# Last recurrent head: the low parts of six mixed tiles move from VectorE to GpSimd, and two output tiles are filled side by side

## The reference, cut to what matters

```python
def hgrn2_mixer(q_raw, f_raw, i_raw, g_raw, lb, norm_g):
    ...
    k = (1.0 - lbf) * jax.nn.sigmoid(-z)
    q = jax.nn.silu(q_raw.astype(jnp.float32))
    v = i_raw.astype(jnp.float32)
    ...
    def chunk_step(state, inp):
        qb, kb, vb, lfb = inp
        b = jnp.cumsum(lfb, axis=2)
        diff = jnp.where(causal, b[:, :, :, None, :] - b[:, :, None, :, :], -jnp.inf)
        scores = jnp.einsum('bhtk,bhsk,bhtsk->bhts', qb, kb, jnp.exp(diff))
        o = (jnp.einsum('bhts,bhsv->bhtv', scores, vb)
             + jnp.einsum('bhtk,bhkv->bhtv', qb * jnp.exp(b), state))
        ...
    o = o * lax.rsqrt(jnp.mean(o * o, axis=-1, keepdims=True) + RMS_EPS)
    o = o.reshape(B, S, HGRN_WIDTH) * norm_g.astype(jnp.float32)
    o = o * jax.nn.silu(g_raw.astype(jnp.float32))
...
    x = x + jnp.concatenate([y_pool, y_hgrn], axis=-1) @ w_out[l]
```

## Time and profile before

| | |
|---|---|
| median of 3 runs | 2525.26 us (2523.75 to 2525.31) |
| the profiled execution | 2528.88 us |
| its span in the trace | 2527.1 us |
| mean granted TensorE clock | 0.994 of full speed |
| TensorE busy | 2480.5 us, 98% of the span |
| VectorE, GpSimd, ScalarE busy | 67%, 45%, 32% |

### The profile page before, as it was taken

The page is one execution under the profiler, slowest core; times in us unless marked ns, Lnnn a source line. Parts: engine busy times, 40 slices in busy tenths (PEclk is TensorE's granted clock), DMA queues, the critical chain, the costliest instruction groups (busy, mean ns, idle before and its releaser), DMA issues.

```text
span 2527.1 us, 38526 instructions
## 1 busy us (share of the span) xinstructions
PE 2480.5 (98%) x14121; PEld 2036.5 (81%) x14121; DVE 1693.6 (67%) x1822; ACT 807.4 (32%) x1137; POOL 1133.0 (45%) x665
## 2 busy tenths in 40 slices
PE   8999998999999999999999999999999999999998
PEld 7788886878888788887877778888878888878886
DVE  6755556753334566668777879454789999986665
ACT  5333344343333000003233331311355445431003
POOL 2322222367876233323322223233379999962333
PEclk9999998999999999999999999999999999999998
DMA  6111112234424322221311101113222222243222
GB/s 211 42 42 33 33 33 93 100 113 122 134 100 148 126 99 92 100 100 42 126 40 40 39 26 50 50 44 132 84 83 83 91 75 91 84 158 108 100 94 81
DMA packets 221471, 217.48 MB, mean 86 GB/s; under 512 B 16304, under 2 KB 185947, under 8 KB 220379
## 3 DMA queue, kind: packets, MB, share of 16 engines
q1 hardware_dynamic: 189604, 122.92, 16.1%
q10 hardware_dynamic: 31798, 93.64, 10.0%
HBM read 167.24 MB, written 51.06 MB: 86 GB/s over the span
## 4 chain that ended last, share of the span: by engine, by line
PE 87%; DVE 8%; ACT 2%; issue 1%; DMA 1%; ACTq 0%; DVEq 0%; SPq 0%
PE psum L849 28%; PE psum L1134 27%; PE psum L868 21%; PE psum L1350 3%; PE psum L888 2%; PE psum L976 1%; PE psum L1279 1%; PE psum L1454 1%; DVE h_lo L2144 1%; DVE sq_sum L2412 1%; PE psum L1260 1%; DVE sq_sum L2139 1%; PE psum L1035 0%; DVE sq_sum L2546 0%; DVE x_t L2420 0%
## 5 line engine op out<-in xcount | busy, mean ns | idle before, releaser
L753 POOL CAST w_hi<-w_raw 128x1024 fp32r<-128x1024 f32 x136 | 152.7, 1123 | 1187.0 <-issue 629.7
L2448 DVE TENSOR_TENSOR x_t<-x_t,psum 128x512 f32<-128x512 f32 x416 | 284.4, 686 | 206.9 <-PE psum L868 198.4
L755 POOL TENSOR_TENSOR w_lo<-w_raw,w_hi 128x1024 fp32r<-128x1024 f32 x136 | 345.8, 2543 | 10.9
L849 PE MATMUL psum<-h_hi,w_hi 128*128 128x512 f32 x1040 | 334.3, 403 | 7.7 <-DVE h_lo L2247 6.5
L849 PE MATMUL psum<-h_lo,w_hi 128*128 128x512 f32 x1040 | 322.6, 392 | 0.0
L849 PE MATMUL psum<-h_hi,w_lo 128*128 128x512 f32 x1040 | 321.6, 390 | 0.0
L849 PEld LDWEIGHTS psum<-h_hi,w_lo 128*128 128x128 f32 x1040 | 196.1, 189 | 42.1
L849 PEld LDWEIGHTS psum<-h_lo,w_hi 128*128 128x128 f32 x1040 | 196.1, 189 | 41.9
L849 PEld LDWEIGHTS psum<-h_hi,w_hi 128*128 128x128 f32 x1040 | 190.0, 189 | 49.1 <-issue 11.8
L868 PE MATMUL psum<-down_hi,w_hi 128*128 128x512 f32 x512 | 200.3, 391 | 2.8 <-DVE x_t L2448 2.6
L868 PE MATMUL psum<-down_lo,w_hi 128*128 128x512 f32 x512 | 199.9, 390 | 0.0
(11 more groups left out here) (448 smaller groups left out, 5558.6 us busy)
## 6 DMA issues: line engine op xcount, KB each, us to landing
w_raw<-in_w_in SPq DMA_DIRECT2D x124, 256.0 KB, 3.2
w_raw<-in_w_down SPq DMA_DIRECT2D x108, 256.0 KB, 2.7
w_raw<-in_w_up SPq DMA_DIRECT2D x76, 256.0 KB, 3.9
act_rows<-mlp_a ACTq DMA_DIRECT2D x32, 512.0 KB, 3.9
down_in<-act_rows ACTq DMA_DIRECT2D x32, 512.0 KB, 3.7
ffn_raw<-in_w_up SPq DMA_DIRECT2D x44, 256.0 KB, 3.5
ffn_rows<-ffn_gate ACTq DMA_DIRECT2D x22, 512.0 KB, 2.6
ffn_in<-ffn_rows ACTq DMA_DIRECT2D x22, 512.0 KB, 3.9
```

The source lines that it names most:

```text
L753: pool.tensor_copy(hi, w_raw[:, slot, :]).then_inc(weight_hi, 1)
L755: pool.tensor_tensor(lo, w_raw[:, slot, :], hi.bitcast(F32), ALU.subtract).then_inc(weight_split, 1)
L849: last = pe.matmul(psum[:, first_bank + t, :], w, a[:, k, t * HALF:(t + 1) * HALF], start=(k == 0 and j == 0), stop=(k == KT - 1 and j == 2))
L2448: dve.tensor_tensor(x_d, x_d, psum[:, 4 + g % 4, :], ALU.add).then_inc(down_added, 1)
```

## The change

Six low parts (tiles 1 to 6) leave VectorE and go to GpSimd, in its list ahead of the split of output tile 2's weights. VectorE keeps tile 0 (right after level 1) and tile 7. ScalarE's high parts are spread over the levels, its gate (`sg_t`) moves from before level 2 to after level 4, and the copy `v_tok` goes ahead of level 4 with tile 3 before it. On VectorE `take_g` moves from behind `move(1)` to behind `merge(1, 5)`, and the product `gated` to behind `merge(3, 5)`; `move(2)` now stands ahead of the diagonal's merge. TensorE fills output tiles 0 and 1 side by side in slots 1 to 6. The number of steps in slots 1 to 3 (eight), 4, 5, 6 and 7 is the same as before. Heads 0 to 4 keep their order.

```diff
@@ GpSimd, split(n, slot, _, skipped)
                 elif isinstance(n, int) and n in (T_OUT1 + 2, T_OUT1 + 3):
+                    if n == T_OUT1 + 2:
+                        for d in range(1, KT - 1):
+                            pool.wait_ge(mix_hi_ready, d + 1)
+                            pool.wait_ge(mix_split, d)
+                            pool.tensor_tensor(h_lo[:, d, :], mix1[:, d, :], h_hi[:, d, :].bitcast(F32), ALU.subtract)\
+                                .then_inc(mix_split, 1)
@@ TensorE
             def begin_rest():
-                begin_out(1, range(5, 7))
+                for t in range(2):
+                    begin_out(t, [6])
                 begin_out(2, range(7))
-            head(HEADS - 1, [lambda: project_g(HEADS - 1), lambda: begin_out(0, range(0, 4)),
-                             lambda: begin_out(0, range(4, 7)), lambda: begin_out(1, [0]), lambda: begin_out(1, [1]),
-                             lambda: begin_out(1, [2, 3]), lambda: begin_out(1, [4]), begin_rest])
+            def begin_both(tiles):
+                for t in range(2):
+                    begin_out(t, tiles[t])
+            head(HEADS - 1, [lambda: project_g(HEADS - 1), lambda: begin_out(0, [0]),
+                             lambda: begin_both(([1, 2], [0, 1, 2])), lambda: begin_both(([3], [3])),
+                             lambda: begin_out(0, [4]), lambda: begin_both(([5], [4])),
+                             lambda: begin_out(1, [5]), begin_rest])
@@ ScalarE, head(h, last), after level(0) and level(1)
-                act.wait_ge(y_ready, h + 1)
-                act.wait_ge(zg_ready, h + 1)
-                act.activation(sg_t[:, :], zg[:, :], ACT.Sigmoid).then_inc(g_gate, 1)
                 if last:
                     act.wait_ge(tile_done, T_OUT1)
-                begin_mix(0, 1)
-                level(2)
-                begin_mix(2, 3, 4, 5, 6)
-                level(3)
...
+                    begin_mix(0, 1)
+                    level(2)
+                    begin_mix(2)
+                    level(3)
+                    begin_mix(3)
+                    values()
+                    level(4)
+                    gate()
+                    begin_mix(4)
+                    level(5)
+                    begin_mix(5, 6)
+                    level(6)
                     act.wait_ge(mix_split, KT - 1)
                     act.dma_start(x_t[:, 0:KT - 1, :].rearrange("p d t -> p (d t)"),
...
@@ VectorE, head(h, last): the branch of the last head
+                if last:
+                    mix_lo(0, 0, mix1)
+                    move(2)
+                    merge_diagonal()
+                    merge(0, 4)
+                    move(3)
+                    merge(1, 5)
+                    take_g(h)
+                    move(4)
+                    merge(2, 4)
+                    move(5)
+                    merge(3, 5)
+                    gated()
+                    move(6)
+                    merge(4, 6)
+                    merge(5, 4)
+                    merge(6, 5)
...
             head(HEADS - 1, True)
+            dve.wait_ge(mix_split, KT - 1)
             mix_lo(0, KT - 1, mix1)
```

More of the change, by code:

```diff
@@ L1583, in head, with gate, values @@
                 act.wait_ge(kd_start, h + 1)
+                def gate():
+                    act.wait_ge(y_ready, h + 1)
+                    act.wait_ge(zg_ready, h + 1)
+                    act.activation(sg_t[:, :], zg[:, :], ACT.Sigmoid).then_inc(g_gate, 1)
+                def values():
+                    act.wait_ge(v_turned, h + 1)
+                    act.activation(v_tok[:, :, :].rearrange("p c v -> p (c v)"), banks(6), ACT.Copy).then_inc(v_ready, 1)
                 level(0)
                 level(1)
-                act.wait_ge(y_ready, h + 1)
-                act.wait_ge(zg_ready, h + 1)
-                act.activation(sg_t[:, :], zg[:, :], ACT.Sigmoid).then_inc(g_gate, 1)
                 if last:
                     act.wait_ge(tile_done, T_OUT1)
-                begin_mix(0, 1)
-                level(2)
-                begin_mix(2, 3, 4, 5, 6)
-                level(3)
-                act.wait_ge(v_turned, h + 1)
-                act.activation(v_tok[:, :, :].rearrange("p c v -> p (c v)"), banks(6), ACT.Copy).then_inc(v_ready, 1)
-                if last:
+                    begin_mix(0, 1)
[10 more added lines that the diff above has]
+                    level(6)
                     act.wait_ge(mix_split, KT - 1)
@@ L1604, in head @@
                                   x_spill[:, 0:(KT - 1) * SEQ]).then_inc(x_back, 16)
-                level(4)
-                level(5)
-                level(6)
+                else:
+                    gate()
+                    level(2)
+                    level(3)
+                    values()
+                    level(4)
+                    level(5)
+                    level(6)
                 act.wait_ge(kd_turned, h + 1)
@@ L2290, in merge, with gated @@
                        .then_inc(level_merged, 1)
[L2292 to L2295, removed]
+                def gated():
+                    dve.wait_ge(g_gate, h + 1)
+                    dve.tensor_tensor(sg_t[:, :], zg[:, :], sg_t[:, :], ALU.mult).then_inc(sg_ready, 1)
                 dve.wait_ge(q_gate, h + 1)
@@ L2304, in head @@
                 move(1)
[L2305 to L2318, removed]
+                if last:
[15 more added lines that the diff above has]
+                    merge(6, 5)
+                else:
+                    take_g(h)
+                    merge_diagonal()
+                    merge(0, 4)
+                    move(2)
+                    merge(1, 5)
+                    gated()
+                    move(3)
                     dve.wait_ge(k_ready, h + 1)
                     take_f(h + 1)
[L2322 to L2329, removed]
+                    merge(2, 4)
+                    move(4)
+                    merge(3, 5)
+                    move(5)
+                    merge(4, 6)
+                    move(6)
+                    merge(5, 4)
                     take_q(h + 1)
-                merge(6, 5)
+                    merge(6, 5)
                 chunk_decay = 2 * SEQ - (2 * SEQ >> LEVELS)
```

## The result

Over 8 runs each, the median went from 2525.45 to 2532.41 us. The ratio of the changed kernel to the one before is 1.0021, 95% interval 1.0012 to 1.0029; a later series (6 runs of the changed kernel, 19 of the one before) gave 1.0030, 1.0018 to 1.0042. Taken together, the two intervals say that the change makes the kernel slower, by 3 to 11 us (0.1 to 0.4%); the forecast of 2532 us, slower, holds.

A forecast was written before the change was run, and what follows sets the result against it. It took the last head to be bound by the start of `o`, behind VectorE's ladder. `o` 6.1 us late by turns with GpSimd, plus 1 us of clock, made 7 us: 2525.26 + 7 = 2532 us, range 2528 to 2537.

The forecast's parts named there:

- What bounds the head: Last head: the start of `o`, 428.85 us before, sets the head's end, which moves by as much.
- The turns: VectorE instructions reading two SBUF tiles and GpSimd instructions alternate; a move of 1.4 us takes 6.1 at level 2.
- The layout: Hand-made schedule of the last head's ladder: last move ends at 427.5 instead of 420.7 us, `o` starts at 435.0.
- 4.9 us too long: Level 5's move between GpSimd's low parts 4 to 6, ending at 418.6 us, takes this much more.
- The clock's share: TensorE at half clock for steps behind the turning of `kd_t`: 0 to 3 us, taken as 1.
- The free edits: Spread high parts, later reload (issued at 419.9 us, landing 12.6 later) and two tiles side by side cost nothing.
- The idle time: TensorE in the last head: some 17 us idle instead of 11.4, with some 5, 5 and 3 us stretches.
- No port cost: Rival, chance 0.07: six low parts run beside the moves; `o` 6 to 9 us earlier, 2518 us.
- VectorE keeps the port through a move: Rival, chance 0.11: GpSimd waits until a move is through; `o` 4 to 6 us earlier, 2520 us.
- Cancelling: Rival, chance 0.09: earlier start and VectorE's shorter list weigh as much as the turns; within 5 us, 2525 us.
- Slower still: Rival, chance 0.11: idle time before the turning brings the clock down through `o` and the mean; 2537 to 2541 us.
- within 0.2%: Chance 0.30 that the median stays within 5 us of before, 2520.2 to 2530.3 us.

The follow-up runs named there:

- e2: The changed kernel with GpSimd's splits of `w_out` tiles 2 and 3 held until `kd_t` is turned: `o` after 41.6 us, ratio to before 1.0002.
- e3: The changed kernel's order on all engines, but low parts 1 to 6 back on VectorE: `o` after 40.9 us, ratio to before 0.9996.
- e6: The kernel before, with only GpSimd's splits of `w_out` tiles 2 and 3 held until `kd_t` is turned: `o` after 37.2 us, ratio 0.9982.
- e1: The changed kernel with GpSimd's six low parts left out, only their counts given: `o` after 35.3 us, ratio to before 0.9984.
- the repetition: The changed kernel once more, unaltered, for a second profile: median 2532.36 us, `o` after 47.6 us.
- e7: The changed kernel with each of GpSimd's six low parts replaced by a `memset` of the same tile: `o` after 36.9 us, timed once, 2525.96 us.
- e8: e5 with the low part of `w_out` tile 1's weights also held until the move of level 2 is done: `o` after 32.3 us, ratio 0.9966.
- e5: The changed kernel with all low parts on VectorE, re-placed, and `w_out` splits 2 and 3 held until `kd_t` is turned: `o` 34.4 us, ratio 0.9978.

## Why the prediction was right

- **What bounds the head.** Right: the start of `o` carried the end. It moved by 7.3 us (428.85 to 436.11), the first addition behind the head by 7.3 and 7.0. The experiments' medians rise with it (only the kernel before and e2 are out of order, by 0.5 us): 32.3, 34.4, 35.3, 37.2, 40.9, 40.9, 41.6 and 48.3 us of head go with 2515.8, 2519.3, 2521.0, 2521.4, 2524.3 (e3), 2525.3 (before), 2524.8 and 2532.4 us. One step was read wrongly: in the kernel before, the turning did not wait for the ladder's last move but for TensorE's own work at half clock, 1.3 us longer (e6). It did not matter for the sum, since in the changed kernel the turning did wait for VectorE.
- **The turns.** Right, and the core of it. The layout had the ladder's last move at 427.5 us, measured 426.6; level 2 with low parts 1 and 2 at 394.1 to 400.2, measured 394.0 to 399.8 (`qd_t` came just ahead of low part 1, so that `kd_t` and `decays` were the ones that waited, not `qd_t` and `kd_t`); `o` at 435.0 without and 436 with the clock, measured 436.1. In the changed kernel's last head too GpSimd went next wherever both waited. e1, e2 and e3 show it by removal: 13.0, 6.7 and 7.4 us of head, each with the 2.0 us of clock; they overlap and don't add up. The prediction's "4.9 us too long" for level 5 does not follow from its own times, which give 5.8 (ready at 411.5, 1.3 us of work, done at 418.6); measured are 5.7. The sum did not use it.
- **The clock's share.** Taken as 1 us inside 0 to 3, measured 2.0. The term was too small, and the ladder's was too large by 0.9; that they cancel to within 0.1 us is luck.
- **The free edits.** Right as far as the profile shows: the reload was issued at 418.15 us, landed 11.2 us later, and nothing behind the head waited for it; idle time before the first addition was 5.21 us, released by TensorE, as before.
- **The idle time.** 17 us forecast, 16.3 measured; 5, 5 and 3 us for the longest, 5.16, 4.23 and 2.82 measured.
- **The rivals.** No port cost is out by e1 (13 us). That VectorE keeps the port through a move is out by the rows of level 6. Cancelling happened only by the numbers of one pair of executions, not in the head. *Slower still* did not come: the clock was back at full speed before `o`.
- **Where it was weakest.** The size against what a measurement can tell. Forecast +7 us on the median; the medians say +7.0, the ratio of the first series +0.21%, 5.3 us, with an interval from 3.0 to 7.3. The 0.30 for "within 0.2%" was not too much. The range of 2528 to 2537 us is wider upwards than its own terms, which reach 2535. And the profiled execution, forecast at 2535.9 us, took 2529.26 and in the repetition 2536.38 us: the chance of some 7 us behind the head stood in no term.

The Trainium skill's "SBUF — State Buffer", section "Who interferes with whom", was confirmed in its finer point as well: a two-input VectorE instruction meets a GpSimd instruction that reads, not one that only writes. In e7 `kd_t` took 0.68 us beside a `memset`, in the changed kernel 2.86 us beside a `tensor_tensor`.

## What to carry to other kernels

Moving a two-input elementwise instruction from VectorE to GpSimd saved VectorE 1.16 us here and cost it up to 2.2 us of waiting per turn, wherever VectorE stood in a chain of two-input SBUF instructions; look which of VectorE's instructions would run beside it, and put GpSimd's reading work beside those that read PSUM (e8) or behind the chain (e2, e5, e6). A lay-out by hand, with the durations of one profile and one rule on who goes next, gave the start of `o` within 1 us for five of the seven kernels that it was made for (e2 and e6 missed by up to 1.7 us), and was good enough to choose a better order. Compare such a change at a point inside the program; 7 us of chance lay behind it. A place where two such instructions start within half a microsecond of each other (2275 us here) makes the time of one and the same kernel jump; ordering them by a semaphore, as e8 does in the head, was not tried there.

## What the runs showed of the hardware

- When VectorE (two SBUF inputs) and GpSimd (a reading instruction) both have work waiting, they alternate instruction by instruction in the changed kernel's last head, even where VectorE's next one is 16 columns wide: 2.35 us for 0.17. Of the three exceptions in the kernel before, all copies, the clear one is that of 408.10 us.
- GpSimd's `memset` of 128x1024 (0.95 us, reads nothing) does not take part in this (e7).
- The stretches at half clock differ between executions of one kernel: 394.1 to 397.5, 400.9 to 411.1 and 424.8 to 431.6 us in the first, 393.0 to 413.5 and 427.2 to 430.6 us in the repetition, while `o` came after 48.3 and 47.6 us. In the ladder TensorE at half speed cost nothing here: 13.6 and 20.5 us at half clock, and the turning started 39.5 us after the head's first matmul in both. With no idle time above 1.72 us in the head (e8) there was no such stretch.
